# Index scatters released by head instead of by the beat of the weight panels, in a two-block transformer kernel

## The chip, the cores and the metric

One core of a Trainium2 chip runs the whole program in one launch. The metric is the device time of one execution in microseconds. Besides the timed runs there is one execution recorded by the hardware profiler, and the rows below come from that one.

## What is computed

Two transformer blocks over 512 tokens of width 1024, in fp32. What matters here is the feed-forward part of the first block, a product-key expert layer:

```
s = einsum('thpd,hpnd->thpn', q, keys)                 # 8 heads, 2 axes, 128 keys
s_top, i_top = top_k(s, 16)
best_s, best_pos = top_k(cand_s, 16)                   # 16 of 256 pairs
eid = take_along_axis(cand_i, best_pos)                # one of 16384 experts
w = softmax(best_s)
act = gelu(einsum('thkd,td->thk', u_tab[eid], x))
y = einsum('thk,thkd->td', w * act, v_tab[eid])
```

The kernel does not gather the rows of `u_tab` and `v_tab` for most tokens. It multiplies all 128 panels (128 experts each) of U with all tokens, applies gelu, and later multiplies V with `gelu * weight`, where `weight` is a dense table (expert x token) that is zero except at the picks. That table lies in device memory (`w_scratch`, `w_d` in the code) and is filled by scatters from the picks. The last 128 tokens are the exception: for them rows of V and their gelu values are gathered.

## The kernel before

**Panels.** Every weight matrix is cut into panels of 128 x 1024. For each panel SyncE issues a load into one of four `raw` slots, ScalarE rounds it into `whi` (L1014), VectorE computes the rest `wlo` (L1534, helper `lo`), and TensorE multiplies three products for each of 8 depth tiles (L478 to L480). Semaphore `lo_ready` counts the `wlo` operations; semaphore `used` counts the panels that TensorE is done with, and both the next `whi` but one and the gelu of that panel wait for it. ScalarE's order in this stage, for each panel: `whi` of the next panel, gelu of this one (L1321), then the issue of its store to `gelu_scratch` (L1324).

**The stage of the change.** From panel WQ on, 16 query panels and then 128 U panels run through TensorE. Beside them VectorE does the picks, written out by hand in one order with the `wlo` operations between them (`next_lo`; `TOPS_AT` fixes after how many panels each head's tops are done). For each of `PH` = 8 heads, `token_picks(h)` computes the offsets into `w_scratch` (`offs`), and the weights (`vals`). For head 0 the three token tiles (`DT` = 3) become ready together (L2072); for later heads each tile needs the operations L2088, L2092, L2095 and L2097, as weights of an expert picked by earlier heads too are added, and L2097 adds one to `pick_ready`. The width of these operations grows with the head's number.

**The scatters.** GpSimd does nothing in this stage but issue indirect DMAs. One scatter (L2446) writes 128 weights of one pick, one per token. Its loop runs over heads, token tiles and 16 picks, 8 x 3 x 16 = 384 scatters, numbered `c`. Before a tile's 16 scatters it waits for `pick_ready`, and, from the second head on, until the scatters of the earlier heads for this tile have landed. Three of every ten scatters also wait until `lo_ready` has reached a count of panels: 22 + 3c/10 panels after WQ (`PACE_AT` = 22). The last head waits besides until all picks are made, and issues 8 gathers of V rows (L2422) between its scatters.

**Afterwards.** SyncE waits for all scatters before it loads the first rows of `w_scratch` (L430), and then panels of V follow. SyncE gets there after its last load of the U panels has been issued. GpSimd goes on with gathers of gelu values (L2429) and V rows once all gelu stores have landed.

Of the kernel before, what the change touches and what calls it, by code (L numbers as in the profile page):

```python
# [39 lines left out]
PH = HP // 2  # L40
# [114 lines left out]
def build(nc, panels, mod2_d, small, xT_d, ctxT_d, rope_d, keys_d, dist_d, w_d, ge_d, out):  # L155
    with ExitStack() as ctx:
# [2246 lines left out]
        @block.gpsimd  # L2403
        def _(pool):
            nc.gpsimd.memset(g_pad[:, :, 0:PAD], 0.0)
            nc.gpsimd.memset(g_pad[:, :, PAD + T:GW], 0.0).then_inc(pad_ready, 1)
            pool.wait_ge(small_in, 16)

            experts = w_d.rearrange("i j (t o) -> (i j t) o", o=1)

            def column(s):
                h, k = s // TOPK, s % TOPK
                at = (h * TT + DT) * TOPK + k
                return slice(at, at + 1)

            gelus_ = ge_d.rearrange("i j (t o) -> (i j t) o", o=1)
            v_table = panels.rearrange("g p n -> (g p) n")

            def gather_row(s):
                if s >= VS:  # L2420
                    pool.wait_ge(v_added, s - VS + 1)
                nc.gpsimd.indirect_dma_start(v_rows[:, s % VS, :], None, v_table,  # L2422
                                             bass.IndirectOffsetOnAxis(vals[:, column(s)].bitcast(U32), 0)).then_inc(vrow_in[s % VS], 16)

            def gather_gelu(s):
                h = s // TOPK
                if s % TOPK == 0 and h >= 2:
                    pool.wait_ge(cw_ready, h - 1)
                nc.gpsimd.indirect_dma_start(g_pick[:, s:s + 1], None, gelus_,  # L2429
                                             bass.IndirectOffsetOnAxis(offs[:, column(s)], 0)).then_inc(gpick_in[h % 2], 16)  # L2430

            pool.wait_ge(zero_out, 16 * ZEROS)
            for h in range(PH):
                if h == PH - 1:
                    pool.wait_ge(picks, picks_made[0])
                for t in range(DT):
                    pool.wait_ge(pick_ready, h * DT + t + 1)
                    if h:
                        pool.wait_ge(scattered[t], 16 * TOPK * h)
                    for k in range((h * TT + t) * TOPK, (h * TT + t + 1) * TOPK):  # L2440
                        c = (h * DT + t) * TOPK + k % TOPK
                        if c % 10 in (0, 4, 7):
                            pool.wait_ge(lo_ready, WQ - U + PACE_AT + c * 3 // 10)
                        if h == PH - 1 and c % (DT * TOPK // VS) == 0:
                            gather_row(c % (DT * TOPK) // (DT * TOPK // VS))
                        nc.gpsimd.indirect_dma_start(experts, bass.IndirectOffsetOnAxis(offs[:, k:k + 1], 0), vals[:, k:k + 1], None)\  # L2446
                          .then_inc(scattered[t], 16)

            for done in ge_out:
                pool.wait_ge(done, 16 * (NK // GE_SLOTS))  # L2450
            for s in range(TOPK):
                gather_gelu(s)
            asked = TOPK
            for s in range(PICKS):
                while asked < min(PICKS, TOPK + 2 * (s + 1), s + AHEAD):
                    gather_gelu(asked)
                    asked += 1
                if s + VS < PICKS:
                    gather_row(s + VS)
# [85 lines left out]
```

## Time and profile before

| what | before |
|---|---|
| median of 3 timed runs | 2541.25 us (2539.21 to 2551.24) |
| the profiled execution, its own time | 2543.47 us |
| its span, first to last instruction | 2541.7 us |
| TensorE busy | 2445.8 us (96%) |
| VectorE busy | 1682.9 us (66%) |
| GpSimd busy | 743.7 us (29%) |
| mean granted TensorE clock | 0.986 |

Busy time is the time in which an engine had an instruction running. The profile divides the span in 40 slices of 63.5 us each and gives each engine's busy share in tenths. Idle time carries the name of what ended it; "remote" and "another core or an unknown queue" mean that the view could name no releaser, and "issue" that the engine waited for nothing the profile shows.

### The profile page before, as it was taken

To read this page: it belongs to the slowest core of one execution; us is meant where nothing else is said; L and a number is where in the kernel's file an instruction comes from. 1 tells how busy PE (TensorE), PEld (TensorE's weight loads), DVE (VectorE), ACT (ScalarE), POOL (GpSimd) and SP (SyncE) were. 2 spreads that over 40 slices of the span, in tenths; PEclk is the share of its full clock that TensorE was granted. 3 is DMA by queue.
4 is the path that set the end of the run, shared out by engine and by line. 5 is a ranking of instruction groups with operands and counts; after the bars stand their busy time and mean duration, and the time that the engine had idled before them with its cause. 6 is when DMAs were issued, how large, how long until landed. Compare 5 with 4: busy or idle time off the path is not lost.

```text
span 2541.7 us, 34943 instructions
## 1 busy us (share of the span) xinstructions
PE 2445.8 (96%) x12016; PEld 2073.1 (82%) x12016; DVE 1682.9 (66%) x3129; ACT 911.3 (36%) x1308; POOL 743.7 (29%) x646
## 2 busy tenths in 40 slices
PE   6999999998999999999999999999999989999998
PEld 4877887786887878888777899999999766788886
DVE  4887768788666676777632378888887784444434
ACT  4223852523233333333322333333333564222222
POOL 0000000000025666666675347777741000000000
PEclk8999999999999999999999999999999999999999
DMA  6322913353234444444455589999997212222231
GB/s 256 100 75 98 341 50 127 138 191 141 83 129 137 140 143 140 149 137 145 139 163 166 191 272 363 366 361 359 361 365 279 83 34 67 91 95 95 99 98 59
DMA packets 177222, 433.60 MB, mean 171 GB/s; under 512 B 32752, under 2 KB 81904, under 8 KB 176752
## 3 DMA queue, kind: packets, MB, share of 16 engines
q1 hardware_dynamic: 123888, 331.61, 38.2%
q0 software_dynamic: 34816, 67.41, 7.6%
q10 hardware_dynamic: 18432, 33.56, 3.5%
q8 instruction: 38, 0.62, 0.1%
q14 instruction: 48, 0.39, 0.0%
HBM read 371.48 MB, written 61.01 MB: 170 GB/s over the span
## 4 chain that ended last, share of the span: by engine, by line
PE 82%; DVE 9%; another core or an unknown queue 3%; issue 2%; ACT 2%; DMA 1%; ACTq 0%; SPq 0%; DVEq 0%
PE ps L478 16%; PE ps L480 16%; PE ps L479 16%; PE ps L829 8%; PE ps L831 8%; PE ps L830 8%; DVE wlo L1534 2%; PE ps L736 2%; DVE ar L1587 1%; PE ps L708 1%; ACT whi L1014 1%; PE ps L726 1%; PE ps L548 1%; PE ps L550 1%
## 5 line engine op out<-in xcount | busy, mean ns | idle before, releaser
L1534 DVE TENSOR_TENSOR wlo<-raw,whi 128x1024 fp32r<-128x1024 f32 x426 | 521.4, 1224 | 605.6 <-ACT whi L1014 515.2
L2446 POOL DMA_INDIRECT w_scratch<-ar x384 | 420.9, 1096 | 953.4 <-DVE wlo L1534 849.2
L1014 ACT ACTIVATE whi<-raw 128x1024 fp32r<-128x1024 f32 x424 | 448.8, 1059 | 662.5 <-PE ps L831 348.9
L478 PE MATMUL ps<-b_hi,whi 128*128 128x512 f32 x1312 | 515.8, 393 | 15.8 <-DVE wlo L1534 15.6
L480 PE MATMUL ps<-b_hi,wlo 128*128 128x512 f32 x1312 | 512.6, 391 | 0.8 <-issue 0.8
L479 PE MATMUL ps<-b_lo,whi 128*128 128x512 f32 x1312 | 512.4, 391 | 0.0
L829 PE MATMUL ps<-a_hi,whi 128*128 128x384 f32 x1024 | 344.4, 336 | 6.1 <-issue 3.7
L831 PE MATMUL ps<-a_hi,wlo 128*128 128x384 f32 x1024 | 343.2, 335 | 0.0
L830 PE MATMUL ps<-a_lo,whi 128*128 128x384 f32 x1024 | 343.2, 335 | 0.0
L478 PE MATMUL ps<-a_hi,whi 128*128 128x512 f32 x808 | 323.3, 400 | 6.0 <-DVE wlo L1534 3.3
L480 PE MATMUL ps<-a_hi,wlo 128*128 128x512 f32 x808 | 316.0, 391 | 0.0
L479 PE MATMUL ps<-a_lo,whi 128*128 128x512 f32 x808 | 315.9, 391 | 0.0
L478 PEld LDWEIGHTS ps<-b_hi,whi 128*128 128x128 f32 x1312 | 247.5, 189 | 74.0 <-DVE wlo L1534 22.9
L480 PEld LDWEIGHTS ps<-b_hi,wlo 128*128 128x128 f32 x1312 | 247.3, 188 | 52.2
L479 PEld LDWEIGHTS ps<-b_lo,whi 128*128 128x128 f32 x1312 | 247.5, 189 | 50.6
L829 PEld LDWEIGHTS ps<-a_hi,whi 128*128 128x128 f32 x1024 | 193.2, 189 | 7.9 <-issue 6.0
L2429 POOL DMA_INDIRECT ar<-gelu_scratch,ar x128 | 171.9, 1343 | 88.1 <-DMA gelu_scratch<-nt 49.3
L830 PEld LDWEIGHTS ps<-a_lo,whi 128*128 128x128 f32 x1024 | 193.2, 189 | 0.0
L831 PEld LDWEIGHTS ps<-a_hi,wlo 128*128 128x128 f32 x1024 | 193.1, 189 | 0.0
L2422 POOL DMA_INDIRECT ar<-panels,ar x128 | 150.4, 1175 | 144.7 <-DVE nt L2158 100.6
L478 PEld LDWEIGHTS ps<-a_hi,whi 128*128 128x128 f32 x808 | 152.7, 189 | 43.0 <-issue 6.5
L479 PEld LDWEIGHTS ps<-a_lo,whi 128*128 128x128 f32 x808 | 152.8, 189 | 33.7 <-issue 2.9
(270 smaller groups left out, 2928.9 us busy)
## 6 DMA issues: line engine op xcount, KB each, us to landing
raw<-panels SPq DMA_DIRECT2D x430, 512.0 KB
w_scratch<-rstd SPq DMA_DIRECT2D x32, 768.0 KB, 10.7
ar<-w_scratch SPq DMA_DIRECT2D x128, 192.0 KB
ar<-gelu_scratch SPq DMA_DIRECT2D x128, 192.0 KB
ar<-mod SPq DMA_DIRECT2D x32, 512.0 KB, 5.3
gelu_scratch<-ar ACTq DMA_DIRECT2D x64, 256.0 KB
gelu_scratch<-sq ACTq DMA_DIRECT2D x32, 256.0 KB
gelu_scratch<-nt ACTq DMA_DIRECT2D x32, 256.0 KB
```

Source lines behind the costliest of these rows:

```text
L478: pe.matmul(bank, w_h, hi[:, k, :], start=(k == 0), stop=False)
L479: pe.matmul(bank, w_h, lo[:, k, :], start=False, stop=False)
L480: last = pe.matmul(bank, w_l, hi[:, k, :], start=False, stop=(k == KT - 1))
L736: last = pe.matmul(ps[:, 6 + hu, t * P:(t + 1) * P], v_tok[:, j, hu * P:(hu + 1) * P], probT[:, t % 2, j, :], start=(j == 0), stop=(j == S ...
L829: pe.matmul(ps[:, d, 0:cols], w_h, hi[:, at, 0:cols], start=first, stop=False)
L830: pe.matmul(ps[:, d, 0:cols], w_h, lo[:, at, 0:cols], start=False, stop=False)
L831: end = pe.matmul(ps[:, d, 0:cols], w_l, hi[:, at, 0:cols], start=False, stop=last)
L1014: act.activation(whi[:, u % SPLIT, :], raw[:, u % RAW, :], ACT.Copy).then_inc(hi_ready, 1)
L1534: dve.tensor_tensor(wlo[:, u % SPLIT, :], raw[:, u % RAW, :], f32(whi[:, u % SPLIT, :]), ALU.subtract).then_inc(lo_ready, 1)
L2422: nc.gpsimd.indirect_dma_start(v_rows[:, s % VS, :], None, v_table, bass.IndirectOffsetOnAxis(vals[:, column(s)].bitcast(U32), 0)).then_in ...
L2429: nc.gpsimd.indirect_dma_start(g_pick[:, s:s + 1], None, gelus_, bass.IndirectOffsetOnAxis(offs[:, column(s)], 0)).then_inc(gpick_in[h % 2 ...
L2446: nc.gpsimd.indirect_dma_start(experts, bass.IndirectOffsetOnAxis(offs[:, k:k + 1], 0), vals[:, k:k + 1], None)\
```

## The change

The wait on the panel beat is kept for the last head only (`h == PH - 1`, head 7). The scatters of heads 0 to 6, 336 of the 384, keep their waits for picks and for earlier scatters, and lose the wait on `lo_ready`.

```
--- before.py
+++ after.py
@@ -2439,7 +2439,7 @@
                         pool.wait_ge(scattered[t], 16 * TOPK * h)
                     for k in range((h * TT + t) * TOPK, (h * TT + t + 1) * TOPK):
                         c = (h * DT + t) * TOPK + k % TOPK
-                        if c % 10 in (0, 4, 7):
+                        if h == PH - 1 and c % 10 in (0, 4, 7):
                             pool.wait_ge(lo_ready, WQ - U + PACE_AT + c * 3 // 10)
                         if h == PH - 1 and c % (DT * TOPK // VS) == 0:
                             gather_row(c % (DT * TOPK) // (DT * TOPK // VS))
```

Scatter number and thresholds: heads 0 to 6 are c = 0 to 335, with thresholds of 22 to 122 panels; head 7 is c = 336 to 383, with thresholds of 122 to 136.

## Rows read from the trace of the kernel before

**Rows 1.** Page, busy time of TensorE and VectorE, slices of GpSimd and TensorE's clock.

```profile
PE 2445.8 (96%) x12016; PEld 2073.1 (82%) x12016; DVE 1682.9 (66%) x3129; ACT 911.3 (36%) x1308; POOL 743.7 (29%) x646
...
POOL 0000000000025666666675347777741000000000
PEclk8999999999999999999999999999999999999999
```

**Rows 2.** Page, the chain that ended last, by engine.

```profile
PE 82%; DVE 9%; another core or an unknown queue 3%; issue 2%; ACT 2%; DMA 1%; ACTq 0%; SPq 0%; DVEq 0%
```

**Rows 3.** Waits: GpSimd, whole span; TensorE and ScalarE, 736 to 1300 us (total, times, longest).

```profile
POOL w_scratch L2446 <- DVE wlo L1534: 849.2, 58, 735.1
...
PE ps L478 <- DVE wlo L1534: 9.1, 10, 2.1
...
ACT ar L1321 <- remote: 30.1, 5, 6.4
```

**Rows 4.** Busy us and instructions of each engine by stretch, clock, DMA share, GB/s.

```profile
640.00:736.00 96.00, 96.00 (x469) 80.70 (x469) 60.77 (x223) 27.87 (x34) 0.00 (x0) 1.00 0.28 93
736.00:1300.00 564.00, 554.71 (x2427) 455.50 (x2426) 385.99 (x1103) 186.76 (x223) 371.99 (x336) 1.00 0.43 141
1300.00:1400.00 100.00, 92.78 (x394) 75.38 (x393) 19.60 (x16) 27.03 (x33) 57.18 (x57) 0.97 0.55 173
...
736.00:817.00 81.00, 78.93 (x342) 64.81 (x341) 52.26 (x183) 25.96 (x31) 48.99 (x49) 0.98 0.42 138
...
977.00:1057.00 80.00, 80.00 (x354) 66.28 (x353) 56.91 (x169) 26.58 (x32) 52.74 (x50) 1.00 0.44 145
```

**Rows 5.** Timeline: a gelu on time, the next one late, TensorE after it.

```profile
855.47 0.60 ACT L1321 ACTIVATE ar<-ps 128x512 f32<-128x512 f32 x1 [3.31 <-PE ps L480]
...
863.98 0.60 ACT L1321 ACTIVATE ar<-ps 128x512 f32<-128x512 f32 x1 [6.38 <-remote]
...
867.49 0.50 PE L478 MATMUL ps<-b_hi,whi 128*128 128x512 f32 x1 [1.18 <-DVE wlo L1534]
```

**Rows 6.** Groups of instructions, 736 to 1300 us: count, busy, mean ns, idle before.

```profile
L2446 POOL DMA_INDIRECT w_scratch<-ar x336 | 372.0, 1107 | 926.9 <-DVE wlo L1534 835.9 <-issue 91.0
...
L1534 DVE TENSOR_TENSOR wlo<-raw,whi 128x1024 fp32r<-128x1024 f32 x101 | 123.7, 1224 | 169.9 <-ACT whi L1014 138.7 <-issue 30.8
```

**Rows 7.** Lines L2446 (all), L1534 (640 to 735, 736 to 1300): ns min/median/max.

```profile
L2446 POOL DMA_INDIRECT w_scratch<-ar x384: 953/962/2766, 736.1 to 1385.1; - x192
...
L1534 DVE TENSOR_TENSOR wlo<-raw,whi x16: 1219/1225/1228, 640.3 to 734.0; 128x1024 fp32r<-128x1024 f32 x16
...
L1534 DVE TENSOR_TENSOR wlo<-raw,whi x101: 1207/1226/1227, 739.4 to 1298.0; 128x1024 fp32r<-128x1024 f32 x101
```

**Rows 8.** Timeline of VectorE: weights of heads 0, 6 and 7, and panel 122.

```profile
725.91 0.18 DVE L2072 COPY ar<-ar 128x48 f32<-128x48 f32 x1
...
1185.38 0.17 DVE L2097 TENSOR_TENSOR ar<-ar 128x16 f32<-128x16 f32 x1
...
1279.81 0.17 DVE L2097 TENSOR_TENSOR ar<-ar 128x16 f32<-128x16 f32 x1
...
1292.46 1.23 DVE L1534 TENSOR_TENSOR wlo<-raw,whi 128x1024 fp32r<-128x1024 f32 x1 [4.40 <-ACT whi L1014]
```

**Rows 9.** Timeline of GpSimd: first scatter, one of the longest, the last head's.

```profile
736.14 1.14 POOL L2446 DMA_INDIRECT w_scratch<-ar  x1 [735.05 <-DVE wlo L1534]
...
1267.26 2.77 POOL L2446 DMA_INDIRECT w_scratch<-ar  x1 [0.30 <-issue]
...
1300.32 0.98 POOL L2422 DMA_INDIRECT ar<-panels,ar  x1 [0.31 <-issue]
...
1308.93 0.97 POOL L2446 DMA_INDIRECT w_scratch<-ar  x1 [2.55 <-DVE wlo L1534]
...
1385.09 0.96 POOL L2446 DMA_INDIRECT w_scratch<-ar  x1 [0.30 <-issue]
```

**Rows 10.** Timeline of SyncE: the first load from the table.

```profile
1403.51 0.34 SPq L430 DMA_DIRECT2D ar<-w_scratch  x1
```

More of the change, by code:

```diff
@@ L2441, in _ @@
                         c = (h * DT + t) * TOPK + k % TOPK
-                        if c % 10 in (0, 4, 7):
+                        if h == PH - 1 and c % 10 in (0, 4, 7):
                             pool.wait_ge(lo_ready, WQ - U + PACE_AT + c * 3 // 10)
```

## The prediction

> **What bounds the kernel now.** I began with the page: TensorE is busy for 2445.8 us of 2541.7, and its clock is at nine tenths or more after the first slice [rows 1]. The chain that ended last gives it 82% and names no GpSimd at all [rows 2]. So a change on GpSimd can only act through something that TensorE waits for. GpSimd's slices show where it works at all: from slice 12 on, and until slice 19 at only 5 to 6 tenths [rows 1].
>
> Next, the waits. GpSimd waited 849.2 us for `wlo` before scatters, but 735.1 us of that is the idle time before its very first one [rows 3]. What the beat really holds back is 114.1 us in 57 waits, 2 us each.
>
> Then the stretches, since the share of an average hides the stage. Before the first scatter, from 640 to 736 us, TensorE is busy for all of 96.00 us. During the 336 scatters that the change touches, 736 to 1300 us, it is busy for 554.71 of 564.00, and from 1300 to 1400 us for 92.78 of 100.00 [rows 4]. The 9.29 us are nearly the 9.1 us in 10 waits for `wlo` [rows 3]. The clock adds something: the stretch 736 to 817 ran at 0.98, so about 0.02 x 81 = 1.6 us [rows 4]. Everything that TensorE could win back in the stage of the change is thus about 9.3 + 1.6 = 10.9 us, 0.43% of the time.
>
> Who makes `wlo` late there? Take one such case [rows 5]. Two gelus start 8.51 us apart, 863.98 after 855.47, and the second had been idle for 6.38 us with a releaser that the view can't name. In ScalarE's order that gelu stands before the `whi` of a later panel, which then makes `wlo` late, and TensorE stands for 1.18 us. GpSimd isn't in that chain. I can't say from this trace what made the gelu late; it is the open point of this prediction. One fact speaks about it: from 977 to 1057 us GpSimd issued 50 scatters at the same rate as elsewhere, and TensorE was busy for 80.00 of 80.00 us [rows 4]. Scatters in themselves don't cost it anything.
>
> **The change part by part.** *What is removed.* Waits of GpSimd for heads 0 to 6: 835.9 us of idle before them ended by `wlo` [rows 6], less the 735.1 us before the first [rows 3], are 100.8 us. A wait's own instruction is within the 0.30 us between two scatters and costs the same with or without.
>
> *What moves.* Each head now starts when its picks are there. Head 0's are at 725.91 + 0.18 = 726.1 us, and it starts some 10 us before the 736.14 of now; head 6's first tile is there at 1185.6 us [rows 8, 9]. A scatter takes 1107 ns in the mean, with 91.0/336 = 0.27 us of issue before it [rows 6], so a head of 48 takes 48 x (1.107 + 0.27) = 66 us. The lower bound is 48 x (0.962 + 0.30) = 61 us, at the median duration [rows 7, 9]. On the beat it is 48 x 0.3 = 14.4 panels at (1298.0 - 739.4)/100 = 5.59 us [rows 7], or 80 us. So a run of GpSimd becomes 14 us shorter for each head, and one rest of about that length takes the place of some seven rests of 2 us. Inside a run the rate rises from 5.59/1.68 = 3.33 to 5.59/1.377 = 4.06 scatters a panel. The number of scatters, their addresses and their bytes are unchanged, so the DMA share of the stage stays at 0.43 [rows 4].
>
> *The last of them.* From head 6's start at 1185.6, 66 us give an end at 1252 us. The kernel before issues the last head's first gather at 1300.32 [rows 9], although `wlo` of panel 122, which it may follow, ended at 1292.46 + 1.23 = 1293.7 and the last weights at 1279.81 + 0.17 = 1280.0 [rows 8]. GpSimd had fallen behind: in head 7's long VectorE operations a scatter took up to 2.77 us [rows 9]. After the change GpSimd is idle there, so the last head starts at 1293.7, 6.6 us earlier. That isn't passed on. At 1308.93 it meets the beat again, which the change keeps, and the last scatter is issued at 1385.09 as before [rows 9]. Nor would it count if it were later: SyncE doesn't reach the table before 1403.51 [rows 10], as it has its loads of panels to issue first. The cover is 1403.5 - 1385.1 - 1.0 = 17 us; a last scatter later by more would hold the first rows of the table, then `weigh`, and the V panels. Value for this part: 0.
>
> *Queued behind.* Nothing new waits. On GpSimd only the scatters and then head 7's gathers are behind the removed waits; no other queue is passed.
>
> *VectorE beside a quicker GpSimd.* `wlo` took 1225 ns (1219 to 1228) in the 16 panels before any scatter, and 1226 ns (1207 to 1227) in 101 panels beside scatters [rows 7]. The one that gives way is GpSimd: 953 ns at least, 2766 ns at most [rows 7]. So a denser run costs VectorE nothing, and I take 0. The other end of the bound: each removed wait lets about one more scatter meet an operation of VectorE, and if each held it for a scatter's full 0.962 us, the 57 of them [rows 3] would be 55 us. Against that stand 169.9 us in which VectorE was idle before its `wlo`s, 1.7 us a panel [rows 6], and most of it would vanish there; what is left I put at 8 us, as the end for this part.
>
> The trace shows the direction of this only for the operations that happened to meet; a rule speaks more sharply against the change. The Trainium skill, page "SBUF — State Buffer", says of the port pair that VectorE and GpSimd share that it is an exclusive lock: whichever starts first has it for its whole instruction and the other fully blocks. By that rule a scatter that starts first would hold a VectorE operation for up to its whole duration, and the sum would be that of the bound above and not 0. The trace agrees on GpSimd's side and shows nothing of it on VectorE's.
>
> *The stalls.* If the late gelus come from how scatters fall against panels, the change redistributes them. Bounds: all gone, -10.9 us; as many again, +10.9 us. As the stage has stretches of 80 us without any at the same rate of scatters, I see no reason for either sign and take 0. From 1300 to 1400 us the 7.2 us lost and a clock of 0.97, 3 us, can fall differently too, as the first gather moves by 6.6 us: another 5 us either way.
>
> *Sum.* 0 + 0 + 0 + 0. Against the profiled execution's own 2543.5 us (span 2541.7 and 1.8 around it) this is 2543.5; that execution lies 2.2 us above the median of the runs, so the time expected is 2541 us.
>
> **The rivals.**
> 1. *No change that can be told* (forecast): 2541 us, within 2531 to 2551.
> 2. *The stalls go.* Were the late gelus caused by the beat itself, which releases a scatter and a panel's work on the same `wlo`, they would vanish with the wait. For it: TensorE lost nothing before the first scatter. Against it: the 80 us without loss, on the beat too [rows 4]. It would give 2541 - 10.9 = 2530, and to pass 0.5% (12.7 us) it needs something of the 7.2 + 3 us after 1300 as well: at best 2541 - 21 = 2520.
> 3. *VectorE is held* (the slower side). Scatters of head h now run at 4.06 a panel through `token_picks(h)` itself, when VectorE is fullest, instead of trailing it on the beat. VectorE would be late with `wlo`, and TensorE would stand. It decides from where the extra hold passes the 1.7 us of idle time a panel, so at two held operations a panel. With 7 heads and some 3 full panels in each, 21 panels x 1 us beyond the cover = 21 us: 2562 us. Against it: the durations [rows 7].
> 4. *More stalls of the known kind*, through a denser train of landings: one more for each present one, +10.9 us, 2552 us; it passes 0.5% only together with stops long enough to lower the clock, as in the stretch at 0.98.
> 5. *The change doesn't act*, because picks and not the beat hold the scatters. It can't be for heads 0 to 5, as 100.8 us of waits show, and it would give the same 2541.
>
> **How the numbers follow.** 0.5% is 12.7 us, about what a measurement of this kernel can tell from no change. Forecast and rival 5 together 0.80, rival 2 0.09 (0.05 of it beyond 0.5%), rival 3 0.04, rival 4 0.07 (0.03 beyond 0.5%). Faster by over 0.5%: 0.05. Slower: 0.04 + 0.03 = 0.07. Within: 0.88. The range takes rival 2's 2530 and rival 4's 2552 as its ends, which are also the bounds of the unknown stalls, and leaves out rival 3 and the parts of 2 and 4 beyond 0.5%, 0.12 together.
>
> **What would show it right or wrong.** In the profile after: first scatter at 726 us and not 736; seven runs of 60 to 67 us with a rest after each; last scatter of head 6 near 1252 us; the last head from 1294 us and its last scatter near 1385 us; idle time of GpSimd in the stage in fewer, longer pieces. `wlo` still at 1.226 us at most 1.23; TensorE busy for 554.7 +- 9 of the 564 us. What would make the prediction wrong: `wlo` or `token_picks` stretched by scatters, which rival 3 needs; ten or more additional late gelus with the clock falling after them; or the last scatter later than 1402 us, so that SyncE stands before L430.

## The result, and the profile after

Four executions of the changed kernel took 2817.75 us in the median (2810.76 to 2820.33), beside 2546.24 us (2539.21 to 2552.63) for four of the kernel before in the same place. A place here is the chip that the runs beside one another were given; it will matter below. The ratio is 1.1052, 95% interval 1.1028 to 1.1075: slower by 271.5 us. The prediction, 2541 us and at most 2552, was wrong.

The profiled execution took 2819.72 us, with a span of 2817.9; before it was 2543.47. Here are the page's busy times, the slices of TensorE, GpSimd and the clock, the chain that ended last, and two groups of instructions; they answer to [rows 1, 2].

```profile
PE 2502.7 (89%) x12016; PEld 2097.0 (74%) x12016; DVE 1681.7 (60%) x3129; ACT 910.6 (32%) x1308; POOL 713.2 (25%) x646
...
PE   6999999989774856849788999999999997999998
...
POOL 0000000000525326152461432777774100000000
PEclk9999999999886978869898999999999999999999
...
PE 74%; another core or an unknown queue 11%; DVE 8%; issue 4%; ACT 2%; DMA 1%; ACTq 0%; SPq 0%; DVEq 0%
...
L2446 POOL DMA_INDIRECT w_scratch<-ar x384 | 392.8, 1023 | 1194.8 <-DVE ar L2072 726.0
L478 PE MATMUL ps<-b_hi,whi 128*128 128x512 f32 x1312 | 532.7, 406 | 157.5 <-issue 81.9
```

The same 12016 matmuls ran. TensorE was busy for 2502.7 us in place of 2445.8, 56.9 more, and idle for 2817.9 - 2502.7 = 315.2 us in place of 95.9, 219.3 more: together the 276.2 us between the two profiled executions. VectorE and ScalarE were busy for as long as before, and GpSimd for 31 us less. So apart from TensorE nobody worked longer; TensorE stood, and its clock fell while it did. The chain's share without a named releaser rose from 3% to 11%, and "issue" from 2% to 4%.

Where it happened is seen in the stretches (the view of [rows 4]; busy us of TensorE, weight loads, VectorE, ScalarE, GpSimd, each with its instructions, then clock, DMA share, GB/s).

```profile
640.00:736.00 96.00, 96.00 (x469) 80.68 (x468) 60.78 (x222) 27.81 (x34) 7.10 (x7) 1.00 0.28 93
736.00:1300.00 564.00, 381.22 (x1488) 296.48 (x1487) 234.06 (x748) 115.06 (x139) 232.51 (x234) 0.80 0.26 87
1300.00:1400.00 100.00, 83.01 (x337) 65.46 (x337) 56.98 (x154) 24.20 (x29) 52.39 (x48) 0.90 0.35 111
```

Up to the first scatters nothing changed. In the 564 us after that TensorE was busy for 381.22 us, not 554.71, with a mean clock of 0.80, and only 234 scatters went out. The rest of the stage came later: SyncE's first load from the table stands at 1674.95 us, 271.4 us after the 1403.51 of [rows 10]. Nearly all of the loss lies ahead of it, and before the weighing and the V panels.

The waits of the same stretch, 736 to 1300 us, against [rows 3] (total, times, longest):

```profile
DVE wlo L1534 <- ACT whi L1014: 316.8, 46, 43.8
POOL w_scratch L2446 <- DVE ar L2097: 207.5, 4, 55.1
ACT ar L1321 <- remote: 105.0, 5, 44.8
...
ACT nt L1321 <- remote: 71.0, 3, 43.4
...
ACT sq L1321 <- remote: 69.4, 4, 31.6
...
PE ps L478 <- issue: 64.2, 22, 13.4
...
PE ps L478 <- DVE wlo L1534: 57.0, 6, 22.5
...
PE ps L480 <- issue: 31.4, 19, 3.6
PE ps L479 <- issue: 29.6, 19, 2.9
```

[rows 3] has one of the three groups of gelus (L1321) that waited for a releaser that the view can't name. The other two of the kernel before are these:

```profile
ACT nt L1321 <- remote: 12.7, 2, 6.4
...
ACT sq L1321 <- remote: 6.1, 1, 6.1
```

So it was 30.1 + 12.7 + 6.1 = 48.9 us in eight cases before, and is now 105.0 + 71.0 + 69.4 = 245.4 us in twelve. That is the late gelu of [rows 5], with the same follow-up: `whi` late, `wlo` late, TensorE idle. But one thing is new: at L478 to L480 TensorE has 64.2 + 31.4 + 29.6 = 125.2 us of idle time in which it waits for nothing that the profile shows, more than twice the 57.0 us in which it waits for `wlo`. How these two go together is seen in the first run of scatters, which began at 727.1 and ended at 789.1 us. The timeline of ScalarE:

```profile
731.82 0.60 ACT L1321 ACTIVATE ar<-ps 128x512 f32<-128x512 f32 x1 [3.31 <-PE ps L480]
...
741.24 0.60 ACT L1321 ACTIVATE sq<-ps 128x512 f32<-128x512 f32 x1 [7.30 <-remote]
...
765.85 0.60 ACT L1321 ACTIVATE sq<-ps 128x512 f32<-128x512 f32 x1 [22.48 <-remote]
...
794.63 0.60 ACT L1321 ACTIVATE nt<-ps 128x512 f32<-128x512 f32 x1 [26.67 <-remote]
```

and that of TensorE at the end of that run:

```profile
781.93 0.59 PE L478 MATMUL ps<-b_hi,whi 128*128 128x512 f32 x1 [2.21 <-issue]
784.73 0.58 PE L479 MATMUL ps<-b_lo,whi 128*128 128x512 f32 x1 [2.21 <-issue]
787.53 0.59 PE L480 MATMUL ps<-b_hi,wlo 128*128 128x512 f32 x1 [2.22 <-issue]
790.33 0.58 PE L478 MATMUL ps<-b_hi,whi 128*128 128x512 f32 x1 [2.21 <-issue]
791.73 0.59 PE L479 MATMUL ps<-b_lo,whi 128*128 128x512 f32 x1 [0.82 <-issue]
792.43 0.79 PE L480 MATMUL ps<-b_hi,wlo 128*128 128x512 f32 x1
793.13 0.79 PE L478 MATMUL ps<-b_hi,whi 128*128 128x512 f32 x1
```

Gelus are 5.44 us apart when all is well. Here they are 9.4, 24.6 and 28.8 apart. Matmuls with operands long there start 2.80 us after one another, for 0.23 us from 640 to 736 us, and after the scatters have stopped 1.40 and then 0.70, until about 794.5 us, from where it is 0.4. Three register instructions of SyncE took 0.70 us each at 770.7 to 773.5 us in the same trace; the median of such an instruction is 0.037 us there. GpSimd meanwhile issued its scatters in 0.96 us every 1.26 us, and VectorE's operations kept their durations. So TensorE's and SyncE's own instructions were slow, and the gelu that waits for a finished panel started up to 23 us late there.

### The profile page after: what moved, and what is told of

The parts are those of the page before. It is cut to its first block, busy times and chain, and to the rows that moved or that the text cites. A ratio compares the mean times of both kernels' runs of the same rounds, so it can differ in the third digit from the quotient of the medians.

```text
span 2817.9 us, 34942 instructions
## 1 busy us (share of the span) xinstructions
PE 2502.7 (89%) x12016; PEld 2097.0 (74%) x12016; DVE 1681.7 (60%) x3129; ACT 910.6 (32%) x1308; POOL 713.2 (25%) x646
## 4 chain that ended last, share of the span: by engine, by line
PE 74%; another core or an unknown queue 11%; DVE 8%; issue 4%; ACT 2%; DMA 1%; ACTq 0%; SPq 0%; DVEq 0%
PE ps L478 15%; PE ps L480 14%; PE ps L479 14%; PE ps L829 7%; PE ps L831 7%; PE ps L830 7%; DVE wlo L1534 2%; PE ps L736 2%; DVE ar L1587 1%; PE ps L708 1%; ACT whi L1014 1%; PE ps L726 1%; PE ps L548 1%; PE ps L550 1%
## 5 line engine op out<-in xcount | busy, mean ns | idle before, releaser
L1534 DVE TENSOR_TENSOR wlo<-raw,whi 128x1024 fp32r<-128x1024 f32 x426 | 521.5, 1224 | 881.8 <-ACT whi L1014 809.8
L2446 POOL DMA_INDIRECT w_scratch<-ar x384 | 392.8, 1023 | 1194.8 <-DVE ar L2072 726.0
L478 PE MATMUL ps<-b_hi,whi 128*128 128x512 f32 x1312 | 532.7, 406 | 157.5 <-issue 81.9
L480 PE MATMUL ps<-b_hi,wlo 128*128 128x512 f32 x1312 | 527.7, 402 | 38.9 <-issue 38.6
L479 PE MATMUL ps<-b_lo,whi 128*128 128x512 f32 x1312 | 527.6, 402 | 35.9 <-issue 35.8
L478 PEld LDWEIGHTS ps<-b_hi,whi 128*128 128x128 f32 x1312 | 255.9, 195 | 227.8 <-issue 88.5
L480 PEld LDWEIGHTS ps<-b_hi,wlo 128*128 128x128 f32 x1312 | 255.7, 195 | 101.8 <-issue 48.3
L478 PE MATMUL ps<-a_hi,whi 128*128 128x512 f32 x808 | 323.2, 400 | 5.9 <-DVE wlo L1534 3.3
L479 PEld LDWEIGHTS ps<-b_lo,whi 128*128 128x128 f32 x1312 | 256.2, 195 | 94.9 <-issue 43.4
L480 PE MATMUL ps<-a_hi,wlo 128*128 128x512 f32 x808 | 316.1, 391 | 0.0
L478 PEld LDWEIGHTS ps<-a_hi,whi 128*128 128x128 f32 x808 | 152.7, 189 | 43.4 <-issue 6.5
```

The source lines that it names most:

```text
L478: pe.matmul(bank, w_h, hi[:, k, :], start=(k == 0), stop=False)
L479: pe.matmul(bank, w_h, lo[:, k, :], start=False, stop=False)
L480: last = pe.matmul(bank, w_l, hi[:, k, :], start=False, stop=(k == KT - 1))
L1534: dve.tensor_tensor(wlo[:, u % SPLIT, :], raw[:, u % RAW, :], f32(whi[:, u % SPLIT, :]), ALU.subtract).then_inc(lo_ready, 1)
```

## The experiments

Two theories in the beginning. **A**: a run of scatters without a break, 1.26 us apart, fills something that signals of other engines pass too. **C**: the scatters, freed from the beat, run through VectorE's picks (rival 3 in another form). Later A was divided: does any break between two scatters help, or is it the rate (**B**)?

It turned out at once that the place where a kernel runs matters too. The kernel before took 2546 us in some places, the one of the result among them, and 2512 to 2514 in others. By the numbers of the chips on record these are chips 13 and 3 for 2546, and chips 15 and 8 for 2512 to 2514; the number of the result's chip isn't on record. Each result below therefore names what the kernel before took beside it. Many are single executions, which is enough for a loss of 250 us and not for one of 10. Of the kernel before there is one trace, from the place of the result. The edits are against the changed kernel; in head0_free and beat_tenth the line shown stands in place of the one that the change touches. In the kernels with a filler the last head also waits until all fillers are done.

**The first four, beside a kernel before of 2514.02 us.** head0_free keeps the beat for heads 1 to 7 and frees head 0 alone; beat_tenth keeps one wait in ten scatters; pause_4 has no beat and lets GpSimd wait, every four scatters and at each tile's end, until the scatters so far have landed; filler lets GpSimd clear 256 unused columns behind each scatter.

```
head0_free:  if h and c % 10 in (0, 4, 7):
beat_tenth:  if c % 10 == 0 or h == PH - 1 and c % 10 in (4, 7):
pause_4:     + if h < PH - 1 and t:
             +     pool.wait_ge(scattered[t - 1], 16 * TOPK * (h + 1))
             ...
             + if h < PH - 1 and k % 4 == 0 and k % TOPK:
             +     pool.wait_ge(scattered[t], 16 * (TOPK * h + k % TOPK))
filler:      + if h < PH - 1:          # behind each scatter
             +     if c:
             +         pool.wait_ge(idled, c)
             +     nc.gpsimd.memset(area(16128, 256), 0.0).then_inc(idled, 1)
```

> Only head 0 loses the beat, heads 1 to 7 keep it. Theory A (an unbroken train of scatters on GpSimd, from about the tenth on, holds back signals and instructions of TensorE and SyncE): one seventh of the loss of 271 us, so about 2585 us, with all of it between 727 and 800 us. Theory B (what hurts is the rate of scatters, 4.1 a panel against 3.3): the same 2585 us. Theory C (the scatters of a head now meet VectorE's weights of the same head, L2088 to L2097): head 0 has none of these operations, so within 5 us of the kernel before.

> The beat is kept for all heads, but one scatter in ten waits for it and not three, so the mean rate is that of the kernel before and the trains are ten long. Theory A: part of the loss comes back, as the tenth scatter of a train is where TensorE's signals began to be late: 2560 to 2650 us. Theory B, with a rate over more than a panel: as before, 2540 to 2550 us. Theory C: as before.

> No beat for heads 0 to 6, but after every fourth scatter GpSimd waits until its own scatters of this tile have landed, a pause of about 1 us; the scatters still follow the picks at once. Theory A: trains of 4 hold nothing back, 2535 to 2555 us. Theory B: the rate falls to 48 scatters in about 73 us, 3.6 a panel, between the two kernels: some 2620 us, and back at the old time only if the limit lies between 3.6 and 4.1. Theory C: scatters fall on VectorE's weights as in the changed kernel, so 2750 us or more.

> The changed kernel with a memset of 256 columns on GpSimd after each scatter of heads 0 to 6; it has no pause between instructions, but the scatters are 1.5 to 1.6 us apart, 3.5 a panel. Theory A in the form that any unbroken work of GpSimd is a train: as slow as the changed kernel or slower, 2800 us or more. Theory A in the form that only DMA issues side by side are a train: 2540 to 2560 us. Theory B: in between, 2560 to 2700 us. Theory C: 2800 us.

Measured: head0_free 2511.74 us, beat_tenth 2513.63, filler 2512.8, and pause_4 2540.59 (ratio 1.0106, 1.0077 to 1.0136). No gelu in the stage waited for an unnamed releaser in any of them. pause_4 lies within the 2535 to 2555 us of theory A by luck: it lost nothing in the stage (its 26.6 us are explained below). Head 0 of head0_free is a free run of 48 scatters in 65.9 us, of the kind that costs the changed kernel dearly, and TensorE was busy for 561.12 of the 564 us. Either the theories were all wrong or the place was another. So the changed kernel was run again.

> The changed kernel once more, unaltered. In the four runs so far a head's unbroken train of 48 scatters at its own pace cost TensorE nothing (head 0 alone freed), while the kernel before itself ran at 2514 us and not 2546 us, without the late gelus in its trace. Theory D (the holding back of TensorE's and SyncE's signals is a property of the place where the first runs were made, chip or session, which unbroken trains of scatters bring out): beside a kernel before at 2514 us it takes 2505 to 2520 us; beside one at 2546 us it takes about 2818 us. Theory A without a place (trains of all seven heads are needed): 2780 us or more even beside a kernel before at 2514 us.

Beside 2546.55 us it took 2806.39, ratio 1.1018 (1.0963 to 1.1074). The loss comes back where the kernel before takes 2546.

**Four in that place, beside 2546.55 us.**

> The changed kernel as a control for the place. Theory D: about 2810 us if the kernel before beside it takes about 2546 us, 2505 to 2520 us if that takes about 2514 us. Theory A without a place: 2780 us or more in both.

> As filler (a memset of 256 columns after each scatter, no pause, 3.5 scatters a panel). Beside a kernel before at 2546 us: if GpSimd's DMA issues side by side make the train, 2540 to 2580 us; if any unbroken work does, 2800 us or more; if the rate decides (theory B), between 2560 and 2700 us.

> As pause_4 (a wait on its own landings after every fourth scatter, no beat). Beside a kernel before at 2546 us, theory A and D (a short pause lets the held signals through): 2545 to 2585 us, as the last head comes later by itself, which cost 27 us beside the kernel before at 2514 us. Theory C (phase against VectorE): 2750 us or more.

> As beat_tenth (one scatter in ten waits for the beat: trains of ten, mean rate as before). Beside a kernel before at 2546 us: theory A, 2560 to 2650 us; theory B with a rate over more than a panel, 2540 to 2550 us.

changed_third (no edit) took 2810.55 us, filler_b 2539.5, pause_4_b 2577.82, beat_tenth_b 2562.18. Two stretches of filler_b, 736 to 1300 and 1300 to 1400 us:

```profile
736.00:1300.00 564.00, 561.20 (x2463) 462.96 (x2462) 387.55 (x1101) 190.12 (x227) 499.60 (x672) 1.00 0.44 145
1300.00:1400.00 100.00, 94.42 (x409) 77.35 (x409) 20.84 (x17) 28.19 (x35) 51.15 (x48) 0.98 0.57 183
```

A memset of 331 ns behind each scatter, no beat at all, and the loss of the stage is gone, even 6.5 of the 9.3 us of the kernel before [rows 4]. The 2.8 us that are left are five waits for `wlo` that head0_free and changed_fifth (below) have as well, where no gelu is late. The shortest distance of two scatters is now 1.46 us. From 1300 us, where the last head has no filler, TensorE loses 5.58 us again. The scatters of filler_b start at 726.7 us and run through the picks like those of the changed kernel, and that falsifies C. Nor are there fewer scatters: their distance differs, and with it what GpSimd does in between.

beat_tenth_b stands between. Its trains reach ten scatters at 1.26 us, and over a head a scatter takes 1.59 to 1.91 us. The same stretch, 736 to 1300 us:

```profile
736.00:1300.00 564.00, 545.93 (x2362) 447.42 (x2361) 383.49 (x1109) 182.46 (x218) 362.85 (x324) 0.98 0.42 138
```

Trains of up to ten cost 8.8 us more of the stage than those of the kernel before, against 173.5 for the changed kernel's, as far as traces from two chips can be compared. The 2562.18 us lie in the 2560 to 2650 of theory A and not in the 2540 to 2550 of B. pause_4_b has trains of four, also 1.26 us apart, and lost no more than filler_b in the stage, yet it is 31 us slower than before (736 to 1300, 1300 to 1400 and 1400 to 1440 us):

```profile
736.00:1300.00 564.00, 561.05 (x2470) 462.92 (x2469) 388.79 (x1113) 189.66 (x227) 339.27 (x296) 1.00 0.44 144
1300.00:1400.00 100.00, 91.83 (x393) 74.64 (x392) 19.68 (x16) 25.53 (x31) 64.06 (x62) 0.97 0.45 147
1400.00:1440.00 40.00, 4.69 (x8) 2.01 (x7) 0.00 (x0) 0.00 (x0) 29.18 (x31) 0.50 0.19 53
```

Its last scatter starts at 1437.4 us, and SyncE, which could load the table from 1403 on, does so at 1439.64; TensorE is busy for 4.69 of 40 us. It is the cover of 17 us that the prediction named, and here it is used up: 1439.6 - 1403.5 = 36.1 us later, 31.3 us on the end. That is also where the 26.6 us of pause_4 come from: last scatter 1425.1, first load 1427.41, while SyncE gets there at 1384.16 in head0_free beside it, and TensorE is busy for 14.97 of the 40 us from 1400 to 1440.

**Is it any break, or the rate?** Four kernels to tell A from B, and whether the size of a scatter counts; they ran beside 2511.93 us. filler_small clears 4 columns, filler_4th clears 256 behind every fourth scatter, half_rows scatters the picks of 64 of the 128 tokens without any beat or filler (half of the table's picks is left out), filler_all puts the filler behind the last head's scatters too.

```
filler_small: nc.gpsimd.memset(area(16128, 4), 0.0).then_inc(idled, 1)
filler_4th:   if h < PH - 1 and c % 4 == 3:
                  if c > 3:
                      pool.wait_ge(idled, c // 4)
                  nc.gpsimd.memset(area(16128, 256), 0.0).then_inc(idled, 1)
half_rows:    n_ = P if h == PH - 1 else P // 2
              ... IndirectOffsetOnAxis(offs[0:n_, k:k + 1], 0), vals[0:n_, k:k + 1] ...
filler_all:   if c:
                  pool.wait_ge(idled, c)
              nc.gpsimd.memset(area(16128 if h < PH - 1 else A_QK, 256), 0.0).then_inc(idled, 1)
```

> The changed kernel with a memset of 4 columns, not 256, after each scatter of heads 0 to 6, so that the issue order on GpSimd is that of filler, but the scatters follow at nearly the full rate of some 4 a panel. Beside a kernel before at about 2546 us (where the changed kernel takes 2810 us): theory A with DMA issues side by side (another kind of instruction between them, with a wait on its predecessor, breaks the train): 2535 to 2555 us. Theory B (rate; filler was fast because its scatters came at 3.5 a panel): 2650 us or more. Beside a kernel before at 2514 us: 2505 to 2520 us in both.

> The memset of 256 columns only after every fourth scatter: trains of four, mean rate some 3.9 a panel. Beside a kernel before at about 2546 us: theory A 2535 to 2560 us, theory B 2650 us or more. Beside one at 2514 us: 2505 to 2520 us.

> The changed kernel, but the scatters of heads 0 to 6 write the weights of 64 of 128 tokens only (half of the table's picks are left out), with half the descriptors and the same 16 landings each. Beside a kernel before at about 2546 us: if the descriptors and their writes are what holds the others back, most of the loss goes, 2540 to 2680 us; if it is the issue and its landings, it stays at 2780 us or more, and more so if a smaller scatter issues faster. Beside one at 2514 us: 2505 to 2520 us.

> As filler, with the memset after the last head's scatters too, which keep the beat. In filler beside a kernel before at 2546 us the only late gelus left (11.5, 8.5 and 7.1 us apart) lay between 1300 and 1350 us, in trains of 6 to 16 on that head. Theory A: they go, TensorE is busy 99 of 100 us from 1300 to 1400, and the time is 2525 to 2535 us. Theory B: the last head's rate isn't changed much, so as filler, 2540 us. Beside a kernel before at 2514 us: 2510 to 2516 us.

They took 2511.13, 2510.91, 2514.05 and 2512.62 us: none shows a gelu that waits for an unnamed releaser, and beside 2511.93 none tells anything apart. head0_free, half_rows, filler_4th and filler_all were not run where the kernel before takes 2546 us, so whether fewer rows in each scatter would help stays open. filler_small got a second run, with the changed kernel beside it:

> The changed kernel again. Beside a kernel before at about 2546 us: 2810 us, the control for the run beside it. Beside one at about 2513 us, where it hasn't been run: theory D says 2508 to 2516 us, as trains of all heads with half the rows took 2514 us there; theory A without a place says 2780 us or more.

> As filler_small (a memset of 4 columns between scatters, nearly the full rate). Beside a kernel before at about 2546 us: theory A with DMA issues side by side 2535 to 2560 us; theory B (rate) 2650 us or more. Beside one at 2513 us: 2511 us again.

Beside 2546.24 us changed_fourth took 2795.35 and filler_small_b 2801.07. The stage of the latter, 736 to 1300 us:

```profile
736.00:1300.00 564.00, 387.92 (x1504) 301.23 (x1504) 237.75 (x764) 116.45 (x140) 262.88 (x470) 0.81 0.27 87
```

and in the view by groups its scatters (L2448 there) and fillers:

```profile
L2448 POOL DMA_INDIRECT w_scratch<-ar x235 | 236.2, 1005 | 234.5 <-DVE ar L2098 189.9 <-issue 44.6
...
L2453 POOL MEMSET ar<- 128x4 f32 x235 | 27.8, 118 | 17.4 <-remote 14.9 <-POOL ar L2453 2.3
```

An instruction and a wait stand between all scatters, as in filler_b, but it is so short (118 ns) that it fits in the pause that was there: scatters are 1.27 us apart at the densest, as in the changed kernel, and the loss is nearly the same. So a break as such is worth nothing, and A in the form of DMA issues side by side (2535 to 2560 us) falls. B, the rate, has its 2650 us or more here. But it doesn't stand as it was put either: it missed filler_b (2560 to 2700 us expected, while the 2539.5 lie just under the 2540 to 2580 of DMA issues side by side) and beat_tenth_b. What is shown is that the distance counts, 1.27 us against 1.46 with the same order of instructions on GpSimd; filler_b's longer memset and the distance can't be told apart in this pair, but pause_4_b has no memset and lost nothing in the stage either.

**The version that might beat both.**

> As filler_all (a memset of 256 columns after every scatter, the last head's too). Beside a kernel before at about 2546 us: theory B (rate; no two scatters closer than about 1.47 us) says that the late gelus between 1300 and 1350 us go, and the time is 2520 to 2535 us, better than filler's 2540 us; if those late gelus come from the gathers of V rows instead, 2538 to 2545 us. Beside a kernel before at 2513 us: 2510 to 2516 us.

It ran beside 2512.94 us and took 2513.67 (median of 8), ratio 1.0004 (0.9993 to 1.0015). Where nothing is lost there is nothing to win. Whether it beats the kernel before where that takes 2546 us wasn't measured. filler_b's 2539.5 beside 2546.55 was a single execution and 0.3% apart, less than can be told here.

**The place by itself, and a rate in between.**

> The changed kernel once more, nothing edited. All its runs so far stood beside a kernel before of about 2546 us and took 2795 to 2820 us; on places where the kernel before takes about 2513 us the changed kernel itself was never run, only kernels with nearly its trains of scatters (2511 to 2514 us). If the loss belongs to the place as well as to the edit: 2790 to 2820 us beside a kernel before of about 2546, and 2510 to 2516 us, with gelus never more than 6.5 us apart between 736 and 1300 us and TensorE busy for at least 558 of 564 us, beside one of about 2513. If it belongs to the edit alone: 2790 to 2820 us beside either.

> After each scatter of heads 0 to 6 GpSimd clears 128 columns (the filler of before cleared 256, the small one 4), and the last head waits for all of it. Scatters should start about 1.32 to 1.40 us apart, between the 1.26 us at which signals were held back and the 1.46 us at which nothing was. If there is an edge near 1.3 us: 2536 to 2550 us beside a kernel before of 2546, TensorE busy for over 555 of 564 us. If the holding back only fades with the interval: 2570 to 2740 us and 420 to 550 of 564 us. If 1.4 us is still too dense: over 2740 us. Beside a kernel before of about 2513 us nothing is expected to differ: 2511 to 2515 us.

Beside 2513.72 us the changed kernel itself took 2512.97 (2511.44 to 2515.17, 8 executions), ratio 0.9997 (0.9985 to 1.0008), and filler_half_b 2514.99. The stretches, and ScalarE in the first run of scatters of changed_fifth:

```profile
736.00:1300.00 564.00, 561.15 (x2471) 463.02 (x2470) 388.83 (x1113) 189.13 (x227) 375.57 (x339) 1.00 0.44 145
1300.00:1400.00 100.00, 100.00 (x443) 82.81 (x442) 23.30 (x19) 30.79 (x37) 49.81 (x49) 1.00 0.60 197
```

```profile
755.63 0.60 ACT L1321 ACTIVATE nt<-ps 128x512 f32<-128x512 f32 x1 [3.31 <-PE ps L480]
761.07 0.60 ACT L1321 ACTIVATE ar<-ps 128x512 f32<-128x512 f32 x1 [3.31 <-PE ps L480]
766.50 0.60 ACT L1321 ACTIVATE ar<-ps 128x512 f32<-128x512 f32 x1 [3.31 <-PE ps L480]
```

The same program, head 0's scatters without a wait from 729.1 to 795.0 us, and each gelu 5.44 us after the one before. Edit and place are needed together. One difference of the two runs looks like a consequence that makes the loss larger: here VectorE keeps working and holds a scatter up now and then, 1.38 us per scatter in head 0; there VectorE stands for want of `whi`, nothing holds a scatter up, and it is 1.30. filler_half_b's scatters stood at least 1.35 us apart, but it didn't get the place in which that would tell something.

The stage in one table: TensorE busy in 736 to 1300 us; the densest ten distances of scatters in a row in the stage (their mean, us); us per scatter over a head, least and most of heads 0 to 6.

| kernel | kernel before beside it, us | us | busy of 564 | densest ten | per scatter |
|---|---|---|---|---|---|
| before | 2546.24 | 2546.24 | 554.71 | 1.34 | 1.64 to 1.71 |
| changed | 2546.24 | 2817.75 | 381.22 | 1.26 | 1.29 to 1.41 |
| filler_small_b | 2546.24 | 2801.07 | 387.92 | 1.27 | 1.37 to 1.49 |
| beat_tenth_b | 2546.55 | 2562.18 | 545.93 | 1.33 | 1.59 to 1.91 |
| filler_b | 2546.55 | 2539.5 | 561.20 | 1.47 | 1.61 to 1.73 |
| pause_4_b | 2546.55 | 2577.82 | 561.05 | 1.41 | 1.83 to 1.98 |
| changed_fifth | 2513.72 | 2512.97 | 561.15 | 1.28 | 1.38 to 1.49 |

In the places with 2546 us the order of the losses is that of the densest ten, and not of the mean rate: filler_b and the kernel before have the same mean. The order hangs on the count, though, which was chosen after the runs: over nine distances beat_tenth_b stands at 1.26 us, as dense as the changed kernel, with a tenth of its loss. What holds whatever the count is coarser. The two kernels that lose over 170 us have trains of up to 25 and 35 scatters (under 1.4 us apart); those with at most ten and seven (beat_tenth_b, before) lose 18 and 9 us of the stage; pause_4_b shows that four at 1.26 us can pass. A theory that fits is something that takes in a scatter's signals, drains more slowly than one in 1.27 us, and holds some ten of them before it holds others back. It is argued from the table; no run shows such a thing, and where its limit lies isn't found. The few late gelus of the kernel before aren't explained by it: one is late at 794.67 us although the densest ten from 736 to 817 us are at 1.54 us, while filler_b at 1.47 has none in the stage. How a scatter falls against a panel may count there; that wasn't tried.

## Why the prediction was wrong

**The step that failed is *The stalls*.** It valued them at 0 within 10.9 us either way, and 271.5 us came. Its argument was a stretch of 80 us without a late gelu "at the same rate of scatters". That was the mean rate of the kernel before, while the prediction's own sum has the rate inside a run rise from 3.33 to 4.06 a panel. Nor is the mean rate the quantity: on the beat a train had 2.5 scatters in the mean and 7 at most, in the changed kernel 7.5 and up to 35 (scatters under 1.4 us apart). Part of that length is itself an effect of the loss, as the same kernel has 3.3 and 11 in changed_fifth. The evidence was from trains of a length that the change does away with. Bounding the step by "as many again" took for granted that stalls are events, each with a price. They weren't: in the first run of scatters three gelus in a row came 9.4, 24.6 and 28.8 us after the one before, and the last of these only when the run was over. The other bound was off too, as 2.8 of the 9.3 us are waits that head0_free and changed_fifth have too. The kind was rival 4's, a denser train of landings, and its direction; its price was 25 times too small. Working it out from [rows 5] was possible only as a question: a gelu 6.38 us late, with a releaser that the view can't name. I left it open and still gave it 0.07. What links dense scatters to TensorE and SyncE stays open, and so does why it happens on some chips: on chip 8 the value 0 was right (ratio 0.9997), and the prediction had no term for that. The last section names a rival that no run settles, the recording of the execution itself.

**The rest of the stage followed the forecast as long as time itself did.** First scatter at 727.07 us for the expected 726; runs of 61.6 to 67.2 us for heads 0 to 6 where 60 to 67 were expected; idle time of GpSimd in few and long pieces (before head 1: 48.78 us). `wlo` is unchanged, 1224 ns in the mean as in [rows 6]. But the end of head 6, expected near 1252 us, came at 1491.6, the last head began at 1551.6 and not 1294, and its last scatter started at 1657.1, not 1385, since the picks are timed by panels and the panels stood. In changed_fifth, where nothing stood, these are 1251.7, 1273.5 and 1366.9 us: the first of them is right to 0.3 us. The 1294 was a misreading: by the code c = 336 isn't one of the three of ten, so the last head's first gather doesn't follow panel 122 but only the last picks, ready at 1280.0 us by [rows 8]; its first wait on the beat is that of c = 337, for panel 123. In changed_fifth the picks were ready at 1272.1 and the gather came at 1272.18. It cost no time.

**VectorE (rival 3 and its rule).** The lock that the Trainium skill describes ("SBUF — State Buffer", section "Who interferes with whom") would have lengthened VectorE's operations. For an operation with two inputs in SBUF, as `wlo` has, the section names only a GpSimd instruction that reads SBUF as a rival, so `wlo` alone is a weak test. But no duration shows it: `wlo` at most 1269 ns, median 1225, in the changed kernel, and VectorE's 3129 operations 1681.7 us together for 1682.9 before. GpSimd's side does show a hold: of the 336 scatters of heads 0 to 6 in the kernel before, all 72 of over 1.2 us overlap a TENSOR_TENSOR of VectorE, and the 68 that overlap no VectorE operation of over 0.15 us took at most 0.98 us. The prediction's bound of 55 us also counted 57 waits where the change removes 52. The loss is not there, and filler_b, with GpSimd busy for 499.60 of the 564 us, has TensorE busy for 561.20.

**The cover of the table.** The prediction put it at 17 us and called the value of the part 0. In the changed kernel the loss moved both sides alike (1657.1 and 1674.95). pause_4 and pause_4_b used the cover up and paid 26.6 and 31.3 us.

**The clock.** The terms of 1.6 and 3 us were of the right kind and far too small. Where TensorE stands, the granted clock falls towards the lower of its two levels, 1.2 of 2.4 GHz: 0.80 in the mean of 736 to 1300 us. Of the 276.2 us between the two profiled executions, 56.9 us are matmuls that ran longer.

**Rival 2**, that the beat itself makes gelus late, has this in its favour: filler_b, without a beat, lost 2.8 us of the stage and not 9.3. But the changed kernel has no beat either and lost 182.8, so the beat isn't what makes gelus late. That the 9.3 us come from the trains between its waits would fit; no run shows it.

## What to carry to other kernels

A wait on the beat of another engine may be the only thing that limits how often an asynchronous instruction signals; before it is removed, ask what else limits the rate, and if nothing does, put in its place something that costs next to nothing, as here a memset of 0.33 us behind each scatter (2539.5 us beside 2546.55), and not a wait for landings (2577.82). A late event whose releaser the trace can't name, in the very stage that a change touches, isn't a fixed price: ask what happens when the longest burst grows and not what the mean rate does, and let the range show that its price is unknown. And run the kernel in more than one place before a difference is believed or dismissed: one edit was worth 271.5 us here and nothing there.

## What the runs showed of the hardware that was not expected

- Indirect scatters of 128 elements, issued 1.26 us apart, 48 to a head, went with a TensorE held back (a matmul every 2.80 us, for 0.23 us when all is well), slow register instructions of SyncE (0.70 us for 0.037) and late signals from TensorE to ScalarE (gelus 28.8 us apart in the first run of scatters for 5.44), while neither GpSimd's scatters (0.96 us) nor VectorE's durations changed. At 1.46 us apart and more it was gone.
- It depends on the place: 2795 to 2820 us for the changed kernel where the kernel before takes 2546, and 2513 where that takes 2513. The 33 us between the two times of the kernel before bear the same mark, as far as a trace shows it: TensorE was busy for 554.71, 92.78 and 253.92 us of 736 to 1300, 1300 to 1400 and 1440 to 1700 us in its own trace, and head0_free, which keeps the beat for seven heads of eight, had 561.12, 100.00 and 260.00 in the other place, 19.7 us more. The rest of the 33 us wasn't followed.
- The trace's own records are thinner there too. Of the 384 x 16 landings of scatters it has 1941 in the kernel before, 1138 in the changed one and 2688 in filler_b, and 6038 in changed_fifth; up to 700 us all four have the same 2608 records of landings. Records of instructions aren't missing: all 12016 matmuls are there in each. The timed executions took as long as the recorded one (2810.76 to 2820.33 beside 2819.72), so that the loss belongs to no single execution. But every timed execution on record comes with a span and a granted clock as well, so none is known to have run without records, and the recording itself is a rival that nothing here rules out. The Trainium skill, "NOTIFIC — the notification-queue block", section 7.1, says that the internal pipeline of the block that writes such records holds its producers back rather than lose a record, and that this path can throttle an engine. Engines that stand for 0.70 us and its multiples would fit that; but records are also missing here, where that section expects none to be lost inside the block, and no run switched them off. What the shared part is, and why places differ, stays open, and so does whether the changed kernel loses anything where nothing is recorded.
